# A transformer layer with mixture of experts on one core: rows of the last two expert units reach their tokens through 0/1 matrices on TensorE

## The reference

```python
def _hier_moe(h, w_group, b_group, w_expert, b_expert, w_gate_exp, w_up_exp, w_down_exp):
    ...
    e_top, e_sel = lax.top_k(jax.nn.softmax(e_logits, axis=-1), EXPERT_TOPK)      # 2 of 8 in the chosen group
    weights = g_top * e_top / jnp.sum(e_top, axis=-1, keepdims=True)
    ...
    for e in range(N_EXPERTS):                                                      # 32
        hid = jax.nn.silu(t @ w_gate_exp[e]) * (t @ w_up_exp[e])                    # width 256
        y = y + combine[:, e:e + 1] * (hid @ w_down_exp[e]).astype(jnp.float32)
...
h_res = (h_res + gate2 * _rms_norm(ffn, g_post_ffn[l])).astype(x.dtype)
```

## Time and profile before

| | us |
|---|---|
| median of 3 runs | 733.14 (731.11 to 736.3) |
| the profiled execution | 730.83 |
| its span, first to last instruction | 728.6 |

### The profile page before, as it was taken

One profiled execution on the slowest core, in us unless ns is written; L12 is line 12 of the kernel. 1 busy time (PEld: TensorE's weight loads), 2 busy tenths in 40 slices (PEclk: granted clock), 3 DMA queues, 4 the chain that ended last, 5 costly groups with the idle time before them and its releaser, 6 DMA issues. The chain is left out here.

```text
span 728.6 us, 7186 instructions
## 1 busy us (share of the span) xinstructions
PE 644.6 (88%) x2514; PEld 319.8 (44%) x2514; DVE 373.5 (51%) x722; ACT 159.8 (22%) x334; POOL 79.5 (11%) x105
## 2 busy tenths in 40 slices
PE   1599999999999999999999989999997999788830
PEld 1455644444455555556644555433433544233310
DVE  4855356998776872337844437823322323122318
ACT  1420111132222222220222220121211212111113
POOL 1013211210011010000000000112121121120010
PEclk9999999999999999999999999999998999999975
DMA  9991806060705042070391059399999999999526
GB/s 327 391 359 34 299 15 231 0 231 0 232 0 197 34 130 103 2 237 29 130 396 81 30 233 400 127 415 421 421 418 423 420 419 421 420 417 413 220 89 264
DMA packets 50132, 171.76 MB, mean 236 GB/s; under 512 B 10032, under 2 KB 10032, under 8 KB 37168
## 3 DMA queue, kind: packets, MB, share of 16 engines
q1 hardware_dynamic: 41824, 154.98, 54.6%
q0 software_dynamic: 5888, 10.52, 3.8%
q10 hardware_dynamic: 2384, 5.80, 2.1%
HBM read 168.13 MB, written 13.63 MB: 249 GB/s over the span
## 5 line engine op out<-in xcount | busy, mean ns | idle before, releaser
L638 PE MATMUL psum<-ring,hT 128*128 128x512 f32 (+1 forms) x576 | 234.4, 560 | 0.0
L638 PEld LDWEIGHTS psum<-ring,hT 128*128 128x128 f32 x576 | 102.6, 190 | 119.1 <-issue 118.7
L912 PE MATMUL psum<-ring,hT 128*64 128x512 f32 (+1 forms) x352 | 85.0, 594 | 4.4 <-issue 4.4
L1608 DVE TENSOR_SCALAR work<-work 128x256 f32<-128x256 f32 x18 | 5.3, 294 | 128.2 <-PE psum L922 101.4
L789 PE MATMUL psum<-ring,hT 128*128 128x512 f32 x128 | 55.8, 593 | 1.6 <-ACT work L1075 0.9
L912 PEld LDWEIGHTS psum<-ring,hT 128*64 128x64 f32 (+1 forms) x352 | 30.0, 142 | 57.2 <-issue 56.2
L1222 DVE SCALAR_TENSOR_TENSOR rows<-ring,sm,rows 128x512 f32<-128x512 f32 x64 | 51.1, 799 | 1.7
L938 PE MATMUL psum<-ring,work 128*64 128x512 f32 (+1 forms) x176 | 46.5, 632 | 4.7 <-issue 4.1
L912 PE MATMUL psum<-rows,hT 128*64 128x512 f32 (+1 forms) x80 | 38.6, 639 | 8.4 <-issue 8.4
L1120 ACT ACTIVATE work<-psum 128x256 f32<-128x256 f32 x18 | 6.9, 383 | 158.9 <-PE psum L912 158.9
L1283 DVE TENSOR_TENSOR both_bufs<-psum,cosT 128x512 f32<-128x512 f32 (+1 forms) x24 | 14.7, 614 | 51.4 <-PE psum L638 39.1
(11 more groups left out here) (249 smaller groups left out, 798.3 us busy)
## 6 DMA issues: line engine op xcount, KB each, us to landing
ring<-in_w_gate_exp SPq DMA_DIRECT2D x22, 1024.0 KB, 20.2
ring<-in_w_up_exp SPq DMA_DIRECT2D x22, 1024.0 KB, 27.4
ring<-in_w_down_exp SPq DMA_DIRECT2D x22, 1024.0 KB, 28.7
ring<-in_w_in SPq DMA_DIRECT2D x8, 2048.0 KB, 9.9
ring<-in_w_ada SPq DMA_DIRECT2D x8, 2048.0 KB, 15.0
ring<-in_w_ada SPq DMA_DIRECT2D x7, 1024.0 KB, 13.9
both_bufs<-in_w_gate_exp SPq DMA_DIRECT2D x5, 1024.0 KB, 22.1
both_bufs<-in_w_up_exp SPq DMA_DIRECT2D x5, 1024.0 KB, 29.9
```

The source lines that it names most:

```text
L638: mm = pe.matmul(o[:, 0:width], hT3[:, k, b * P:(b + 1) * P], w[:, k, :], start=(k == 0), stop=(k == KD - 1))
L912: mm = pe.matmul(o[rows, :], XT[u % 2][:, k, rows], both(SLOT_OF[place])[:, k, :, :], start=(k == 0), stop=(k == KD - 1))
```

## The change

Only units 0 to NS - 1 = 15 are scattered to `y_dram`. Units 16 and 17 (`DIRECT = 2`) keep their results in `YO[0]` and `YO[1]`.

1. **0/1 matrices.** `select` on DVE, after unit 8, writes for each of the two units and each token block a matrix of 128 x 128: 1 where the row's token is the column's. `collect` on PE multiplies these with `YO` and sums both units in PSUM, four products of 128 x 128 by 128 x 512 for each token block, after `down(17)`.
2. **Blanks.** The pairs of these two units would be unset in `y_dram`, so POOL scatters rows of zeros there (`blank`, two indirect transfers ahead of `scatter(2)`); DVE sets the zeros after `tok_ready`.
3. **Readback earlier.** POOL waits for the scatters of units 0 to 15 and for the blanks, and sets `y_base` then. The four transfers are issued by SP instead of ACT, into two slots of `ring` that unit 15 has left (`YG`).
4. **DVE's tail.** The sum of the two pairs becomes `pairs(b)`: blocks 0 and 1 ahead of `downed(17)`, blocks 2 and 3 behind it. `combine(b)` now adds PSUM to that sum, and waits for `collect`.
5. **Overflow earlier.** On PE, ACT and DVE `each_overflow` stands behind unit 15 instead of behind unit 17, ahead of `gate_up(17)` on PE; SP's waits for `down(15)`.

The core of the diff:

```diff
+DIRECT = 2
+NS = NU - DIRECT
+YG_SLOTS = [SLOT_OF[p] for p in UNITS[NS - 1]]
...
-            sp.wait_ge(y_mm, 2 * NU)
+            sp.wait_ge(y_mm, 2 * NS)
...
+            each_overflow(sp, lambda: None, overflow)
+            sp.wait_ge(y_base, 1)
+            rows = y_dram.rearrange("(b p j) d -> b p j d", b=NB, j=2)
+            for b in range(NB):
+                sp.dma_start(YG[b], rows[b]).then_inc(y_back[b], 16)
...
+            def collect(u, b):
+                for n in range(2):
+                    mm = pe.matmul(ps[SUM_BANK[b] + n][:, :], SEL[u - NS][:, b * P:(b + 1) * P],
+                                   YO[u % 2][:, n * 512:(n + 1) * 512], start=(u == NS), stop=(u == NU - 1))
+                if u == NU - 1:
+                    mm.then_inc(sel_done, 1)
...
                 down(u)
+                if u == NS - 1:
+                    each_overflow(pe, settled, overflow)
+            pe.wait_ge(sel_ready, 1)
...
+            collect(NS, 0)
...
+            pe.wait_ge(y_evV, NU)
+            collect(NS + 1, 0)
+            for b in range(1, NB):
+                collect(NS, b)
+                collect(NS + 1, b)
...
-            act.wait_ge(y_base, 1)
-            rows = y_dram.rearrange("(b p j) d -> b p j d", b=NB, j=2)
-            for b in range(NB):
-                act.dma_start(YG[b], rows[b]).then_inc(y_back[b], 16)
...
+                v.memset(BLANK, 0.0).then_inc(blank_ready, 1)
...
+            def select():
+                dve.wait_ge(blank_out, 16 * DIRECT)
+                link(v.tensor_copy(tok_f, tok_t[:, NS:NU]))
+                for i in range(DIRECT):
+                    for b in range(NB):
+                        ins = v.tensor_scalar(SEL[i][:, b * P:(b + 1) * P], cst[:, C_IOTA:C_IOTA + P], float(b * P),
+                                              tok_f[:, i:i + 1], ALU.add, ALU.is_equal)
...
+            def pairs(b):
+                y = YG[b]
+                dve.wait_ge(y_back[b], 16)
+                v.tensor_tensor(y[:, 0, :], y[:, 0, :], y[:, 1, :], ALU.add)
...
+                if u == NU - 1:
+                    pairs(0)
+                    pairs(1)
                 downed(u)
+                if u == NS // 2:
+                    select()
...
             def combine(b):
                 y = YG[b]
-                dve.wait_ge(y_back[b], 16)
-                relay(v.tensor_tensor(y[:, 0, :], y[:, 0, :], y[:, 1, :], ALU.add), y_sum, b + 1)
+                dve.wait_ge(sel_done, b + 1)
+                at = SUM_BANK[b] * 512
+                relay(v.tensor_tensor(y[:, 0, :], y[:, 0, :], psum[:, at:at + D], ALU.add), y_sum, b + 1)
...
+                if u == FIRST_UNITS:
+                    pool.wait_ge(blank_ready, 1)
+                    for direct in range(NS, NU):
+                        blank(direct)
+                if u < NS:
+                    scatter(u)
+            pool.wait_ge(y_out[0], 16 * (NS // 2))
+            pool.wait_ge(y_out[1], 16 * (NS // 2))
+            pool.wait_ge(blank_out, 16 * DIRECT)
```

More of the change, by code:

```diff
@@ L63 @@
 RING = 4
+YG_SLOTS = [SLOT_OF[p] for p in UNITS[NS - 1]]
+assert NS % 2 == 0 and len(YG_SLOTS) == 2 and all(s < RING for s in YG_SLOTS)
 CHUNK = KD * 512
@@ L946, in _, with settled @@
             late_rows()
[L947 to L953, removed]
+            def settled():
+                pe.wait_ge(xt_ev, 2 * NU)
+                pe.wait_ge(hid_ready, NS + 1)
+                pe.wait_ge(ht_ev, NS)
+                pe.wait_ge(y_evA, NS)
+                pe.wait_ge(y_evV, NS)
             def overflow(o):
@@ L973, in overflow @@
                     for i in range(KF):
[L974 removed]
+                        mm = pe.matmul(ps[6 + n][:, :], HT[0][:, i, :], down_of(YG_SLOTS[0])[:, i, n * 512:(n + 1) * 512],
                                        start=(i == 0), stop=(i == KF - 1))
                 mm.then_inc(ov_y, 1)
+                pe.wait_ge(ov_evA, o + 1)
+                pe.wait_ge(ov_evV, o + 1)
+            def collect(u, b):
[4 more added lines that the diff above has]
+                    mm.then_inc(sel_done, 1)
+            for u in range(NU):
+                if u + 1 < NU:
+                    gate_up(u + 1)
+                turn_hid(u)
+                if u + 2 < NU:
+                    turn_x(u + 2)
+                down(u)
+                if u == NS - 1:
+                    each_overflow(pe, settled, overflow)
+            pe.wait_ge(sel_ready, 1)
+            pe.wait_ge(xt_ev, 2 * NU)
+            pe.wait_ge(y_evA, NU - 1)
+            pe.wait_ge(y_evV, NU - 1)
+            collect(NS, 0)
+            pe.wait_ge(hid_ready, NU)
+            pe.wait_ge(ht_ev, NU)
             pe.wait_ge(y_evA, NU)
             pe.wait_ge(y_evV, NU)
[L979 removed]
+            collect(NS + 1, 0)
+            for b in range(1, NB):
+                collect(NS, b)
+                collect(NS + 1, b)
         @block.scalar
@@ L1136, in downed, with settled, overflow @@
                              scale=row_wt[:, u:u + 1]).then_inc(y_evA, 1)
+            def settled():
+                act.wait_ge(hid_ready, NS)
+                act.wait_ge(y_mm, 2 * NS)
+                act.wait_ge(y_out[0], 16 * (NS // 2))
+            def overflow(o):
+                act.wait_ge(ov_turned, o + 1)
+                for q in range(2):
+                    ins = a.activation(XT[0][:, 4 * q:4 * q + 4, :],
+                                       ps[2 + q][:, :].rearrange("p (k c) -> p k c", k=4), ACT.Copy)
+                ins.then_inc(ov_brought, 1)
+                act.wait_ge(ov_gu, o + 1)
+                a.activation(EG[1], ps[4][:, 0:F], ACT.Exp, scale=-1.0).then_inc(ov_exp, 1)
+                act.wait_ge(ov_ht, o + 1)
+                a.activation(HT[0].rearrange("p i c -> p (i c)"), ps[HT_BANK][:, 0:KF * P], ACT.Copy).then_inc(ov_htev, 1)
+                act.wait_ge(ov_y, o + 1)
+                act.wait_ge(ov_ix, o * 3 + 3)
+                a.activation(YO[0][:, 0:512], ps[6][:, :], ACT.Identity, bias=zero, scale=over_wt).then_inc(ov_evA, 1)
+                act.wait_ge(ov_out, o * 16 + 16)
             turned(0)
@@ L1147, in _ @@
                 downed(u)
[L1149 to L1163, removed]
+                if u == NS - 1:
+                    each_overflow(act, settled, overflow)
             a.activation(yr, eps.to_broadcast([P, NB]), ACT.Sqrt, bias=eps).then_inc(tail_root, 1)
             act.wait_ge(tail_root, 1)
-            act.wait_ge(y_base, 1)
-            rows = y_dram.rearrange("(b p j) d -> b p j d", b=NB, j=2)
-            for b in range(NB):
-                act.dma_start(YG[b], rows[b]).then_inc(y_back[b], 16)
             for b in range(NB):
```

69 lines of the change are left out of this document (42 added, 27 removed).

## The result

| | median us | lowest to highest | runs |
|---|---|---|---|
| before | 733.14 | 731.11 to 736.3 | 6 |
| after | 727.59 | 726.17 to 729.51 | 6 |

The ratio is 0.9926 with a 95% interval of 0.9901 to 0.995: some 5.5 us less, 0.7%. The forecast was 728.0, within 1% of before. The profiled execution took 726.17 us with a span of 724.0, 4.6 us less than before's 728.6.

A forecast was written before the change was run, and what follows sets the result against it. Weight DMA sets the pace to 673 us, then a dependent chain leaves PE and DVE idle for 10.16 us. Starting `combine(0)` 5.1 us earlier, blanks' 0.5 us included, gives 733.14 - 5.1 = 728.0 us; range 724.0 to 732.5.

The forecast's parts named there:

- The bound: Near the end, 700 to 710.16 us: neither PE nor DVE works for 10.16 us; the change aims at this.
- The weight stream: In the DMA-bound stretch: two added blanks cost about 0.5 us, bounds 0 and 1 us, shifting all that follows.
- Edits at nothing: Memset, blank issues, `select` and overflow checks hide in idle time; uncovered, the first three would cost 0.9, 2 and 2.5 us.
- The readback: Behind unit 15's scatter: SP issues at about 691.55, block 0 lands at 696.35, the last at 703.8.
- DVE in order: DVE's tail: `downed(17)` 0.3 us late, `pairs(3)` 703.8 to 705.0, so `combine(0)` can start at 705.0.
- PE's sums: After `down(17)`: 3.43 us a block, block 0 done at 703.2, PE ahead of DVE every time.
- The sum: At the end: `combine(0)` moves from 710.16 to 705.0, 5.1 us gained, the 15.35 us behind it kept.
- PE as the gate (1): At block 0's sum: readback ready before it, unit 15's scatter landing within 5.5 us; 7.0 us gain, 726.1; chance 0.17.
- The new wait (2): On DVE: late readback holds `downed(17)` and PE's sums; if 3 us late, 2.1 us gain left, 731.0; chance 0.14.
- No stall at PE's jump (3): Behind unit 15: stalled code fetch makes `gate_up(17)` 6.9 us late, a loss of 1.8 us, 734.9; chance 0.05.
- The clock (4): In PE's sums: half clock makes them 27.4 instead of 13.7 us, end 6.8 us later, 739.9; chance 0.04.

The follow-up runs named there:

- read_late1: Changed kernel with the readback released only when `down(16)` has ended too, against the kernel before: 731.66 us, ratio 0.9988.
- read_late2: Changed kernel with the readback released only when `down(17)` has ended, against the kernel before: 735.55 us, ratio 1.0035.
- blank_thrice: Changed kernel with the pair of blanks issued three times, ahead of the scatters of units 2, 4 and 6, against the kernel before: 730.83 us, ratio 0.9962.
- pe_extra4: Changed kernel with four more unused products on PE ahead of the sums, against the kernel before: 729.47 us, ratio 0.995.
- after_again: The changed kernel itself, run again in another group, against the kernel before: 728.64 us, ratio 0.9938.
- after_third: The changed kernel itself, run once more in a further group, against the kernel before: 729.49 us, ratio 0.9957.
- combined: Changed kernel with POOL's overflow-count load ahead of its scatter wait, `pairs(3)` behind `weigh(0)`, memset behind `gate(0)`, against the kernel before: 727.84 us, ratio 0.992.

## Why the prediction was right, point by point

- **The bound.** Right. The 10.16 us without work were the place, and the readback's landing is what stands in the chain now; read_late1 and read_late2 show that its delay is passed on: 3.7 and 7.1 us by the medians for 4.2 and 8.1 us at the issue.
- **The weight stream.** The right sign, half the size: this is the term of the sum that was furthest off. Predicted 0.5 us for the two blanks, within bounds of 0 and 1; measured 1.04 (the profiles against before's) and 1.08 a pair (blank_thrice). The term was worked out from the share of time that the scatters' own packets took the earlier trace rows. That row was taken where the DMA engines were mostly idle, and it averages over three scatters; those of units 16 and 17 alone moved 0.10 MB in 288 packets. What an indirect write takes from a full stream was not in it. Why it is twice as much stays open.
- **Edits at nothing.** The memset, `select` and the issues on POOL are hidden, as predicted. But the memset had a second effect that I had not seen, on POOL's gather, itself hidden by the stream. The check on PE did not even use the 1.75 us of waiting: PE's queue ran it while the products of `down(15)` were still at work until 682.0:

```profile
L502 PEldq TENSOR_LOAD <-ctl x1: 497/497/497, 678.4 to 678.4; - x1
...
L503 PEldq COMPARE_BRANCH  x1: 243/243/243, 679.3 to 679.3; - x1
```

- **The readback.** Unit 15's scatter landed 7.6 us after its issue (7.5 predicted), the issue on SP came at 692.37 (691.55), block 0 landed 4.8 and block 3 12.2 us after the first issue, as before. Of the 0.8 us by which the issue was late, 0.6 are the stream's.
- **DVE in order.** `downed(17)` at 700.80, held 0.4 us by `pairs(1)` (0.3 predicted). `pairs(3)` ends and `combine(0)` starts at 705.8 (705.0). From there to the end of the last `finish` 15.2 us (15.35).
- **PE's sums.** 14.00 us for the 32 instructions, 3.43 a block, at a granted clock of 1.00; ready near 703.9 for block 0 (703.2). "PE is ahead every time" held, but by a good deal less than block 0 suggests: pe_extra4 found some 0.7 us. The prediction's own list had it, block 1 ready at 706.6 and asked for at 707.5.
- **The sum.** 4.4 us at `combine(0)` where 5.1 was predicted, the blanks being 0.5 us of the difference. By the medians 5.5. That the median came out at 727.59 beside 728.0 is closer than the working deserves and in part luck: a median of the changed kernel moved between 727.6 and 729.5, and at `combine(0)` the sum was 0.7 us too hopeful. It also took the way to unit 15's scatter as fixed, where two further profiles of the same kernel have it 0.8 and 1.0 us longer.
- **The rivals.** PE as the gate (1) did not come: the scatter landed no sooner than before. The new wait (2) did not come, and read_late2 shows what it would have done. No stall at PE's jump (3): the branch took 0.243 us on DMA engines still 68% busy, where the Trainium skill, Runtime: NRT & Kernel Launch, section Instruction fetch mechanics, has a fetch by DMA if the target lies outside the window. No packet of an instruction queue shows from 675 to 684 us, so that case was not met. The clock (4) stayed at 1.00 in the sums. read_late2 shows what rival 4 would have cost: behind 7.50 us of waiting the clock was 0.53 for 3.4 us and then 1.00 again, and `combine(1)` waited 0.51 us. The prediction's 6.8 us, with half the clock through all the sums, was far too much for a wait of this length.

## What to carry to other kernels

Where the last producer's result must go out to memory and come back, send the bulk around earlier and let only the last part take a path on chip. What the step is worth is then set by the landing of the transfer that was moved ahead, and not by the new products; delay that landing on purpose to see it. When two engines hand over blocks, look at the tightest pair of blocks, not at the first: PE's slack was 1.9 us on block 0 and under 1 us on block 1. And a transfer moved ahead hangs on an earlier step, whose own spread (here the 10.0 to 11.1 us from `gate_up(16)` to `down(15)`, by the granted clock) then reaches the end.

## What was not expected of the hardware

- A memset of 128 x 1024 on DVE, 0.91 us, lengthened an indirect DMA instruction on POOL that started 0.12 us after it from 0.99 to 1.80 us, in all eleven profiles with the memset there, and not in the two with the memset later. The Trainium skill, SBUF — State Buffer, section SBUF: two separate sides, says that DVE in some modes locks POOL out of a shared pair of ports, so that POOL cannot write the descriptors of its transfers. Its section Who interferes with whom leaves DVE instructions with at most one SBUF input, outside those modes, out of that, and gives memset as an exception for another chip alone. Here a memset without any SBUF input went with 0.81 us of delay, so the measurement goes beyond the page; it does not show the lock itself, nor in which mode the memset ran.
- A pair of indirect writes for units of few rows (0.10 MB in 288 packets, by the scatters of units 16 and 17 before) went with a full DMA stream 1.04 to 1.08 us longer, where the share of time of such packets on mostly idle DMA engines gives 0.5 or less.
- In three profiles (after_again, after_third, combined) SP's first reload came at 470.1 to 470.6 us, in the others at 466.8 to 468.4. The last `finish` ended at 724.9, 726.2 and 723.6 in these three, against 721.0 in after, so that 2.5 to 3 us of the later end lie ahead of the weight stream. The runs of the changed kernel spread by 3.3 to 4.9 us in its three groups; that before's runs have the same step is likely, but its one profile does not show it.
- Behind waits of 3.6 to 7.5 us on PE the granted clock was low for the first 3.2 to 3.4 us of products: 0.53 in the sums of read_late1 and read_late2, and in `gate_up(16)` 0.71 in before, 0.59 in after and 0.50 in after_third. Not every such wait does it: in after, PE's products at 554.77 us follow a wait of 3.60 us and ran at 1.00. So the same kernel has it in one execution more than in another.
